# Operand reloads of three matrix-multiply stages rounded and split at other products and in halves, and one quadrant sum kept in a scratch row

## The reference

```python
# block 1 (4096 hidden columns) and block 3 (4096 hidden columns, same form)
m = rmsnorm(h, norm_mlp_g[l]) @ w_mlp_up[l]
h = h + jnp.square(jax.nn.relu(m)) @ w_mlp_down[l]
# block 2 (2816 hidden columns)
h = rmsnorm_2(x, ln2_g[l])
x = x + (jax.nn.silu(h @ w_gate[l]) * (h @ w_up[l])) @ w_down[l]
```

## Time and profile before

| | us |
|---|---|
| median of 3 runs | 4531.74 |
| lowest, highest | 4526.34, 4538.97 |
| the profiled execution | 4538.75 |
| its span in the trace | 4536.7 |

### The profile page before, as it was taken

One profiled execution on the slowest core, in us unless ns is written; L12 is line 12 of the kernel. 1 busy time (PEld: TensorE's weight loads), 2 busy tenths in 40 slices (PEclk: granted clock), 3 DMA queues, 4 the chain that ended last, 5 costly groups with the idle time before them and its releaser, 6 DMA issues. The chain is left out here.

```text
span 4536.7 us, 47120 instructions
## 1 busy us (share of the span) xinstructions
PE 3799.0 (84%) x17562; PEld 3124.9 (69%) x17562; DVE 2810.1 (62%) x3066; ACT 1620.2 (36%) x2163; POOL 1433.8 (32%) x1128
## 2 busy tenths in 40 slices
PE   9975999888889986767999988889943978998886
PEld 8953777677668776645777767668733957776765
DVE  3676677666754555464676675654767546776665
ACT  2403333333422233244322233353154543333332
POOL 1110355444412210101344444422210413554443
PEclk9987999899999998878999989999966989998998
DMA  3311143433233312532122333222272532444441
GB/s 129 100 43 37 54 147 134 167 121 112 97 121 111 129 63 49 148 114 80 57 83 91 101 138 113 85 79 80 95 170 48 148 131 72 152 142 146 140 142 53
DMA packets 433719, 478.75 MB, mean 106 GB/s; under 512 B 106228, under 2 KB 321780, under 8 KB 433496
## 3 DMA queue, kind: packets, MB, share of 16 engines
q1 hardware_dynamic: 424136, 441.56, 30.4%
q10 hardware_dynamic: 9360, 34.21, 1.9%
HBM read 324.13 MB, written 151.57 MB: 105 GB/s over the span
## 5 line engine op out<-in xcount | busy, mean ns | idle before, releaser
L190 POOL TENSOR_TENSOR w_wlo<-w_raw,w_whi 128x1024 fp32r<-128x1024 f32 x52 | 136.7, 2628 | 630.7 <-ACT w_whi L184 630.7
L788 POOL TENSOR_TENSOR c_whi<-c_tot,c_whi 128x512 fp32r<-128x512 f32 (+1 forms) x132 | 197.9, 1499 | 346.7 <-ACT c_whi L643 346.7
L788 POOL TENSOR_TENSOR c_wlo<-c_raw,c_wlo 128x512 fp32r<-128x512 f32 (+1 forms) x124 | 199.5, 1609 | 190.3 <-ACT c_wlo L643 190.3
L831 PE MATMUL c_acc<-c_hi,c_whi 128*128 128x512 f32 x420 | 179.9, 428 | 78.9 <-DVE c_hi L1019 40.7
L831 PE MATMUL c_acc<-c_hi,c_wlo 128*128 128x512 f32 x412 | 171.5, 416 | 60.7 <-DVE c_lo L1102 37.5
L190 POOL TENSOR_TENSOR c_wlo<-c_raw,c_whi 128x1024 fp32r<-128x1024 f32 x39 | 100.7, 2581 | 381.4 <-ACT c_whi L184 381.4
L831 PE MATMUL c_acc<-pair,c_whi 128*128 128x512 f32 x466 | 187.6, 403 | 27.1 <-DVE pair L1102 25.8
L219 PE MATMUL c_acc<-c_hi,w_whi 128*128 128x512 f32 x480 | 193.0, 402 | 12.4 <-POOL w_wlo L190 12.4
L219 PE MATMUL c_acc<-pair,w_whi 128*128 128x348 f32 (+1 forms) x512 | 177.1, 346 | 20.6 <-POOLq L164 20.6
L643 ACT ACTIVATE c_whi<-c_tot 128x512 fp32r<-128x512 f32 (+1 forms) x132 | 82.2, 623 | 304.0 <-PE c_acc L834 304.0
L220 PE MATMUL c_acc<-c_lo,w_whi 128*128 128x512 f32 x480 | 188.1, 392 | 0.0
(11 more groups left out here) (744 smaller groups left out, 11553.6 us busy)
## 6 DMA issues: line engine op xcount, KB each, us to landing
hidden<-c_hi SPq DMA_DIRECT2D x172, 256.0 KB, 2.9
c_lo<-hidden SPq DMA_DIRECT2D x37, 1024.0 KB, 8.6
pair<-hidden SPq DMA_DIRECT2D x33, 1024.0 KB, 5.6
hidden<-c_lo SPq DMA_DIRECT2D x129, 256.0 KB, 2.8
proj<-c_tot ACTq DMA_DIRECT2D x49, 512.0 KB, 2.6
w_raw<-in_w_in SPq DMA_DIRECT2D x48, 512.0 KB, 4.6
c_tot<-in_w_ff SPq DMA_DIRECT2D x32, 512.0 KB, 5.3
c_raw<-in_w_ff SPq DMA_DIRECT2D x32, 512.0 KB, 4.7
```

Of the source, the lines that this page charges most:

```text
L190: pool.tensor_tensor(s.wlo[b][:, 0:kt, :], raw[:, 0:kt, :], s.whi[b][:, 0:kt, :].bitcast(F32), ALU.subtract).then_inc(s.lo[b], 1)
L788: pool.tensor_tensor(slot[:, 4:4 + kk, :], factor(n, i), F(slot[:, 0:kk, :]), ALU.subtract)\
L831: pe.matmul(out, slot[:, k, :], hi[:, k, :], start=fresh and k == 0, stop=False, skip_group_check=not fresh)
```

## The change

It has three parts.

**The sum of the fourth product in an up pair** is written back to r1 (`c22`), without the wait for `kept`. That wait now stands after product 4, in front of the scaling, which reads r1 and writes to `Y`. ACT overwrites r1 at the next pair only after `pre` tells that this scaling is done.

**The order of down pairs** is `DOWN`: the seventh product (A22) now comes before the sixth (S4). The last weight sum stays behind the product at r = 5.

**The reloads.** ACT rounds at the products of `UPPER_AT`, 2, 3, 4, 6, 7, 8, 9, where the places count in the order `DOWN`. DVE subtracts in two halves (two k of four each) at the products of `LOWER_AT`, and PE waits for the first half ahead of k = 0 and for the second ahead of k = 2.

```diff
-USUAL, FINAL = (0, 1, 2, 3, 4, 5, 6), (0, 1, 2, 3, 6, 4, 5)
-REFILL = (3, 4, 6, 8, 9, 11, 12)
+USUAL, DOWN, FINAL = (0, 1, 2, 3, 4, 5, 6), (0, 1, 2, 3, 4, 6, 5), (0, 1, 2, 3, 6, 4, 5)
+UPPER_AT = (2, 3, 4, 6, 7, 8, 9)
+LOWER_AT = ((2, 3), (3, 4), (5, 5), (6, 7), (7, 8), (9, 9), (10, 11))
...
-    order = lambda n: FINAL if n == N - 1 else USUAL
+    order = lambda n: USUAL if n < NA else FINAL if n == N - 1 else DOWN
...
+            for p in range(7):
+                soon = p == 0 and fetched[nth]
+                upper_at.setdefault(divmod(7 * n + (-4 if soon else UPPER_AT[p]), 7), []).append((nth, p))
+                for side in range(2):
+                    at = side - 4 if soon else LOWER_AT[p][side]
+                    lower_at.setdefault(divmod(7 * n + at, 7), []).append((nth, p, side))
...
                             elif n:
-                                act.wait_ge(s["c22"], n)
+                                act.wait_ge(s["pre"], 3 * n - 2)
...
-                        for nth, i in refill_at.get((n, r), ()):
+                        for nth, p in upper_at.get((n, r), ()):
+                            i = DOWN[p]
...
-                    if begins(n):
-                        pe.wait_ge(s["op_lo"], 7 * chunk(n) + i + 1)
...
+                        if begins(n) and k in (0, 2):
+                            pe.wait_ge(s["op_lo"], 14 * chunk(n) + 2 * (q % 7) + k // 2 + 1)
...
                     if i == 3:
+                        dve.wait_ge(s["u3"], n + 1)
+                        tt(r1[:, :], r1[:, :], bank(n, 3), ALU.add).then_inc(s["c22"], 1)
+                    if i == 4:
                         dve.wait_ge(s["kept"], 112 * (tile if not gated else tile // 2))
-                        y = to[:, 1, :]
-                        dve.wait_ge(s["u3"], n + 1)
-                        tt(y, r1[:, :], bank(n, 3), ALU.add).then_inc(s["c22"], 1)
                         dve.wait_ge(s["c22"], n + 1)
-                        scale(y, inv[:, 1, :])
+                        scale(to[:, 1, :], r1[:, :], inv[:, 1, :])
...
-                        if i == 5 and n + 1 < N:
+                        if r == 5 and n + 1 < N:
                             weight_sum(n + 1, 4)
...
+                            kk = slice(2 * side, 2 if side == 0 else chunks[nth][1])
+                            dve.wait_ge(s["op_hi"], 7 * nth + p + 1)
+                            tt(lo[:, kk, :], F(lo[:, kk, :]), F(hi[:, kk, :]), ALU.subtract).then_inc(s["op_lo"], 1)
```

More of the change, by code:

```diff
@@ L499, in refills @@
         return nth if n >= NA and (n - NA) % 4 == 3 and nth < len(chunks) else None
-    refill_at = {}
+    upper_at, lower_at = {}, {}
     for n in range(N):
@@ L504, in back @@
         if nth is not None:
-            for i in range(7):
-                at = -4 if i == 0 and fetched[nth] else REFILL[i]
-                refill_at.setdefault(divmod(7 * n + at, 7), []).append((nth, i))
+            for p in range(7):
[4 more added lines that the diff above has]
+                    lower_at.setdefault(divmod(7 * n + at, 7), []).append((nth, p, side))
     with stage(nc, name, *BACK) as s:
@@ L611, in _ @@
                             refill(0, 6)
-                        if nth is not None and not (r == 0 and fetched[nth]) and not (r == 6 and nth == 0):
-                            sp.wait_ge(s["fin"], 7 * n + r + 1)
-                            refill(nth, r)
+                        if nth is not None:
+                            i = order(n)[r]
+                            if not (i == 0 and fetched[nth]) and not (i == 6 and nth == 0):
+                                sp.wait_ge(s["fin"], 7 * n + r + 1)
+                                refill(nth, i)
                         if r == 3:
@@ L1031, in evict_up @@
                         dve.wait_ge(s["c12"], n + 1)
-                        scale(y, inv[:, 1, :])
+                        scale(y, y, inv[:, 1, :])
                     if i == 6:
@@ L1036, in evict_up, with scale @@
                         dve.wait_ge(s["c21"], n + 1)
-                        scale(y, inv[:, 0, :])
-                def scale(y, by):
+                        scale(y, y, inv[:, 0, :])
+                def scale(y, of, by):
                     if gated:
-                        tt(y, y, by, ALU.mult).then_inc(s["pre"], 1)
+                        tt(y, of, by, ALU.mult).then_inc(s["pre"], 1)
                     else:
-                        stt(y, y, 0.0, by, ALU.max, ALU.mult).then_inc(s["pre"], 1)
+                        stt(y, of, 0.0, by, ALU.max, ALU.mult).then_inc(s["pre"], 1)
                 def evict_down(n, i):
@@ L1095, in _ @@
                             weight_sum(n + 1, 3)
-                        if i == 5 and n + 1 < N:
+                        if r == 5 and n + 1 < N:
                             weight_sum(n + 1, 4)
[L1098 to L1103, removed]
+                        for nth, p, side in lower_at.get((n, r), ()):
+                            hi, lo = moving(NA + 4 * nth, DOWN[p])
+                            kk = slice(2 * side, 2 if side == 0 else chunks[nth][1])
+                            dve.wait_ge(s["op_hi"], 7 * nth + p + 1)
+                            tt(lo[:, kk, :], F(lo[:, kk, :]), F(hi[:, kk, :]), ALU.subtract).then_inc(s["op_lo"], 1)
                         if n > N - 4 and r in (2, 4):
```

## The result

The changed kernel took 4308.97 us in the median of 4 runs (4301.8 to 4310.96), the kernel before 4535.35 us beside it: a ratio of 0.950, interval 0.948 to 0.952. The profiled execution took 4307.43 us (span 4305.4), 231.3 us less than that of before. The forecast was 4298 us, range 4258 to 4352.

A forecast was written before the change was run, and what follows sets the result against it. In the seven-product parts, PE's 253 us in 87 waits for reloads and fourth-product sums were counted. 88.6 + 12 + 103.5 + 20.7 + 9.6 = 234 us off 4538.75 gives 4305, as a median 4298; range 4258 to 4352.

The forecast's parts named there:

- Part 1: Up pairs: fourth product's sum no longer waits for the stores; 88.6 us in steady pairs, 12 us in two first ones.
- Part 2: Eight reloads of later chunks: earlier rounding leaves DVE's own queue late next; 103.5 us less.
- 4b: Block 1's second chunk: second half of the subtraction for operand 4, counted from 0; expected 0.4 us late for PE.
- 5a: Block 1's second chunk: first half of the subtraction for operand 5, counted from 0; expected 3.65 us late for PE.
- the 24 to 27 us given: Sign to look for: length of the first pair of a later chunk, where operands are reloaded.
- VectorE and GpSimd hold each other up: Rival, reloads: halves let POOL's splits in front of DVE; about 60 us more, 4358 us; chance 0.12.
- DVE keeps up: Rival, reloads: fewer meetings, clock stays 1.00, pairs near 20.5 us; 40 us less, 4258 us; chance 0.14.
- the other two: Rivals: first reload gives its gain back, 4334 us, 0.09; slower, stores' wait holds ACT and PE, about 4550, 0.03.
- Part 3: First reload of each block, last up and first down pairs: 20.7 us less, between 0 and 36.
- Part 4: Last down pairs: the swap lets the fourth product's sum be needed one product later; 9.6 us less.

The follow-up runs named there:

- the kernel with the filling POOL: The changed kernel with POOL filling the low half of a weight slot with zeros in down pairs instead of subtracting; 4247.31 us, one run.

## Why the prediction was right, and where it was off

**Part 1 held to half a microsecond.** The steady up pairs lost 88.2 us for 88.6, all that there was: a clean pair takes 19.04 us, not 19.03. The wait for the stores is hidden, as worked out, behind the fifth and sixth products. The first up pairs of blocks 1 and 3 lost 5.8 and 5.4 us, 11.2 for 12, and the 4.9 us of waiting that were to stay are there, because DVE itself is late.

**Part 2 is the mis-sized term: 95.3 us for 103.5.** The five with an early fetch went from 38.5 to 38.9 us each to 25.4 to 26.6 (64.4 us for 68.5), block 2's last from 31.7 to 19.1 (12.6 for 9). The two unfetched went from 39.1 and 39.0 to 29.8 and 30.0, where I had taken 26: 18.3 us for 26. The step that failed is the price of a half, 1.17 us, half of a pair of adds that met no split. It holds only for a half that does not begin behind a running split. PE in block 1's second chunk, at the starts of the third product, of the fifth's second half and of the sixth:

```profile
933.48 0.47 PE L838 MATMUL c_acc<-pair,w_wlo 128*128 128x512 f32 x1 [1.28 <-DVE pair L1109]
...
944.84 0.50 PE L838 MATMUL c_acc<-c_hi,w_wlo 128*128 128x512 f32 x1 [2.37 <-DVE c_lo L1109]
...
948.71 0.47 PE L838 MATMUL c_acc<-c_hi,w_whi 128*128 128x512 f32 x1 [2.22 <-DVE c_lo L1109]
```

I had 4b 0.4 us late and 5a 3.65; 4b is 2.37 us late, because six of the nine halves ahead of it had taken 2.09 to 2.33 us, and the third product waits 1.28 us for an operand that I called early. That is also why PE waits 95 us for reloads and not 60, and why these two pairs miss the 24 to 27 us given.

The prediction also took it that stalls under 2.7 us leave the clock at 1.00. The product in that row had waited 2.59 us. In the changed kernel's pair at 1013.60 the granted clock was at 1.00 when PE waited 1.81 us, up to 1027.77, and stood at the lower level, 1.2 GHz, from 1028.53 to 1035.36. So the length of a stall alone does not tell. PE's two waits there, 1.81 and 1.57 us, make about half of the 6.7 us that this pair takes beyond a clean one; the rest is slower products, the sixth at 4.6 us.

**The rival "VectorE and GpSimd hold each other up" had the right mechanism and the wrong price.** It put 60 us on top of the forecast. The meetings do cost about 62 us, but against a kernel without them; the forecast's reload pairs already held most of that: 303.0 us before, less 103.5, is 199.5, against 162.7 without meetings. The rival "DVE keeps up", with pairs near 20.5 us and 4258 us, is what the kernel with the filling POOL showed: 20.7 us and 4247. Of the other two nothing came: the first reloads kept 19.7 us, and the steady up pairs took 19.04. By the Trainium skill, page "SBUF — State Buffer", section "Who interferes with whom", a VectorE instruction with two SBUF inputs contends with a GpSimd one that reads SBUF, not with one that only writes it, and the order of issue decides who is held. The runs agree in all three: 2.32 us behind a split, 1.22 beside a fill; and the half waits where the split began first.

**Part 3: 19.7 us for 20.7.** The last up and first down pair went from 69.1 to 61.1 us in block 1 and from 68.6 to 61.3 in block 3; block 2's first down pair from 46.7 to 42.3. The one long wait came where it was put, at the sixth product, 11.05 us for about 10. Its transfer took 5.6 us from the issue at 850.43 to ACT's start at 856.03, for the 6 taken. I did say that the operand is needed a product earlier in the new order, but not that this costs 16 us in all, which the kernel with the old order in the first down pair shows.

**Part 4: 9.4 us for 9.6.** The two late pairs of block 2 went from 35.0 us to 30.1, and the clock there from 0.95 to 1.00; blocks 1 and 3 gave 4.5 us.

Sum: 88.2 + 11.2 + 95.3 + 19.7 + 9.4 = 223.8 us of the 224.0 by which the blocks' parts fell, against 234. The profiled execution was put at 4305 us and took 4307.4: 10 us less gained, 8 of them in part 2, and 7.3 us got back, by luck, in parts that the change does not touch. The median lies 1.5 us above that execution, where I had put it 7 below, as it was before; this makes the rest of the 11 us between forecast and result.

## What to carry to other kernels

Price an instruction twice, alone and behind what it will meet, before cutting it into pieces: a half that began behind a running split took 2.16 us in the mean instead of 1.21, and the earlier start on halves brought no time. When a long queue is reordered, look for the one element with a deadline of its own; here one order for all down pairs was right for the rest and cost 16 us in the three first ones. And when a wait is moved behind work that covers it, what it cost can be read off beforehand from pairs that never waited.

## What was not expected of the hardware

That the loss goes by who begins first, and that the reordering turned this around: behind a subtraction a split took up to 3.35 us and DVE lost almost nothing, behind a split a half took up to 2.33 us. Whole subtractions at the new places pay as well: 25 of 70 began behind a running split and took 3.02 us in the mean, the others 2.28 or 2.29. So the length of the pieces is not what decides it. The 147 halves took 240.7 us of DVE beside splits and 177.1 beside fills. That this difference, 64 us, lies near the 62 us that the kernel gains without the meetings is not shown to be more than chance, since adds lose time in them too and not every loss holds PE up. And that POOL's filling of a slot, which reads nothing, left VectorE at 1.22 us throughout.
